# A second trunk that starts 16 steps earlier beside a stream of expert rows, its gated blocks first

## The chip, the cores and the metric

The kernel runs on one core of a Trainium2 chip. The metric is the device time of one execution in microseconds. All tensors are float32.

## What is computed

One inference step of a two-layer decoder for two groups of tokens (512 prompt rows, 64 sample rows). Each layer adds three things to the residual rows `x`: a mixer, a cross-attention, and PEER, a lookup of single-neuron experts:

```
q = t @ w_pq                                  # 8 heads, 2 halves of 128
s1, i1 = top_k(s[:, :, 0], 16); s2, i2 = top_k(s[:, :, 1], 16)     # s = q @ sub_keys
cand = s1[..., :, None] + s2[..., None, :]; top_s, pos = top_k(cand, 16)
idx = (i1 * 128 + i2)[pos]; g = softmax(top_s)                     # 128 experts per row
out = sum_e g[e] * gelu(t . peer_u[idx[e]]) * peer_v[idx[e]]
```

The mixer multiplies one normed input by `w_in` (seven parts of 1024 columns: b, c, h for a short convolution, u and v for the gated branch, and two gates), then by three more 1024x1024 matrices. `v` goes through gelu and a layernorm, `u` through gelu.

## The kernel before

**Trunks and the stream.** The work is cut into four passes `p`: for each of two layers, tiles 0 and 1 (256 rows), then tiles 2, 3 and 4 (320 rows). The dense part of a pass is its *trunk*; its PEER part is a stretch of one long *stream*. A *pick* `m` is one of the 128 experts of each of a tile's 128 rows: POOL (GpSimd) gathers the 128 rows of `peer_u` (one indirect DMA of 512 KB into one of eight `urow` slots) and of `peer_v` (another into one of eight `vrow` slots). Pass 0 has picks 0 to 255, pass 1 the next 320, 1152 in all. The trunk of pass 1 runs beside the stream of pass 0, and so on. Only trunk 0 has no stream beside it.

**A step of the stream.** At step `m` DVE (VectorE) computes `dot(m)`, a product and row sum of `urow` with the normed row, at line 1781. ACT makes weights (`w_done`) of four dots at a time. The weighted row of pick `m - LAG` (`LAG` = 8) is added either on DVE (`sum_up`, line 1797) or on PE (TensorE), as two matmuls with a diagonal matrix (line 1049). `plan_sums` gives picks 0 to 39 to PE, and 40 to 200 to DVE. POOL goes in order: before `urow` of pick `m` it waits for dot `m - 8`, before `vrow` of pick `v` for the sum of pick `v - 8`, which frees the slot.

**What sets the order.** Each engine's order is fixed when the program is written. `phase_jobs` lists the matmul jobs of a trunk, `places` gives each a step of the stream (`AHEAD`; `STARTS` is the place of the job ahead of it). An engine that comes to a job calls `peer_to(place)` first and so does the stream's work up to that step. PE does this at the end of each job with the `STARTS` of the next one, and only for its sums. DVE and ACT do it ahead of taking a job's result (line 1520 is ACT's copy out of a PSUM bank), so a result that is ready early stays in its bank until its step, and for one that is late the engine waits with the stream behind it. On DVE, `v` is taken `LATE_GELU` = 4 steps after its place.

**The start.** Trunk 0 ends with the scores (`sc`) of eight heads. In the second half of this tail, blocks of two queries (`pq`) and one score alternate, with scores of heads 2 to 7 at steps 5, 11, 15, 19, 24 and 29. The top-k of tile 0 (`top_group`) goes by head groups 0, 1, 2-3, 4-5 and 6-7, in nine parts each, within the windows between these steps. Trunk 1 begins at step `FIRST` = 40 with `par` (a transpose of parameter rows, whose DMAs SP issues once score 7 is done), norms (`n`), `v`, then blocks c, h, b, u twice, with `lg` and `lb` (layernorm rows spread over the partitions by PE, line 1112) behind the first c. DVE takes `lg` at step 61 and `lb` at step 63. The top-k of tile 1 (`top_k`, in 18 parts) is spread over steps 40 to 104.

**Weights.** SP (SyncE) loads them in units of 2 MB into two slots of `W`, in order; a unit is loaded when PE has finished the unit two before it.

Of the kernel before, what the change touches and what calls it, by code (L numbers as in the profile page):

```python
# [25 lines left out]
KC = DM // P  # L26
# [15 lines left out]
BLK = 4  # L42
# [9 lines left out]
FIRST = 40  # L52
HEAD = 40
# [51 lines left out]
def topk_window(p, i):  # L105
# [7 lines left out]
    return step_base(p) + FIRST, step_base(p) + FIRST + WIDE  # L113
# [27 lines left out]
def first_tail():  # L141

    jobs = [(at[:-1], "dve" if at[0] == "xo" else "act", 2 if at[0] in ("xo", "sk", "n") else 1, 1) for at in FIRST_TAIL]
    for h in range(2, PH):
        jobs += [(("pq", c), "act", 1, 1) for c in queries_before(h)] + [(("sc", h), "act", 2, 1)]
    return jobs


def phase_jobs(p):
# [23 lines left out]
    if not p:  # L173
        jobs += [(("sw",), "dve", 2, 1)]
    for a in range(2):
        jobs += block("c", a, "act")
        if a == 0 and p:
            jobs += [(("lg",), "dve", 2, 1), (("lb",), "dve", 2, 2 * nt)]
        jobs += block("h", a, "dve") + block("b", a, "dve") + block("u", a, "act")
# [69 lines left out]

def places(p):  # L250
# [4 lines left out]
    if p == 0:  # L255
        score = {("sc", h): (0, 0, 5, 11, 15, 19, 24, 29)[h] for h in range(PH)}
# [5 lines left out]
    begin, end = step_base(p - 1) + (FIRST if p == 1 else LAG + 2), step_base(p)  # L262
    if p % 2:
# [80 lines left out]
def plan_units(index):  # L344
# [10 lines left out]
    for p in range(2 * DEPTH):  # L355
        g = p % 2
        nt = len(GROUPS[g])
        for n in range(2):
            add(p, "v", n, "v", nt - 1)
        for a in range(2):  # L360
            for kind in "chbu":
# [74 lines left out]
def decoder_step(nc, A, O):  # L436
# [20 lines left out]
    with ExitStack() as ctx:  # L457
# [312 lines left out]
        def head_window(p, k):  # L770

            ends = [AHEAD[p, "sc", h + n - 1] for h, n in head_groups(p)] + [FIRST if p == 0 else step_base(p) + CARRY if carries(p) else step_base(p) - OVER]
# [186 lines left out]
        def _(pool):  # L959
# [31 lines left out]
            for m in range(STEPS_IN_ALL):  # L991
                if m == NU:
                    pool.wait_ge(job_done, JOB[0, "xo", 1] + 1)
                    for v in range(NV):
                        gather_values(v)
# [6 lines left out]
                if m >= LAG + NV:  # L1002
# [4 lines left out]
        def _(pe):  # L1007
# [186 lines left out]
            def trunk(p):  # L1194
# [33 lines left out]
                for a in range(2):  # L1228
                    for kind in "chbu":
                        for c in range(BLK * a, BLK * a + BLK):  # L1230
                            project((p, kind, c), c, hT)
                        if kind == "c" and a == 0 and p:
                            pe.wait_ge(ln_in, 32 * (p + 1))
                            spread((p, "lg"), LN_ROW, 2 * KC, 0)
                            spread((p, "lb"), LN_ROW, 2 * KC, KC)
# [147 lines left out]
                for h in range(0 if p else 2, PH):  # L1383
                    for c in queries_before(h):
# [18 lines left out]
        def _(act):  # L1403
# [52 lines left out]
            asides += [(step_base(1) - 8, copy_beside, ())]  # L1456
            asides.sort(key=lambda a: a[0])
# [64 lines left out]
            def trunk(p):  # L1522
# [55 lines left out]
                n = ncols(g)  # L1578
                if p:
                    act.wait_ge(idx_done, turns_to(p - 1, len(GROUPS[(p - 1) % 2]) - 1 if g == 0 else 0))  # L1580
                for a in range(2):
                    for c in range(BLK * a, BLK * a + BLK):
                        evac((p, "c", c), F1[:, c, 0:n], pf((p, "c", c)))
                    for c in range(BLK * a, BLK * a + BLK):
                        evac((p, "u", c), F2[:, c, 0:n], pf((p, "u", c)), ACT.Gelu_apprx_tanh)
# [123 lines left out]
                for h in range(0 if p else 2, PH):  # L1709
                    for c in queries_before(h):  # L1710
# [8 lines left out]
                    for k, (h0, some) in enumerate(head_groups(p)):  # L1719
                        if k and h == h0 + some - 1:  # L1720
                            group_exps(p, k - 1)
                k = len(head_groups(p)) - 1
                peer_to(head_window(p, k)[1] - 1)
                group_exps(p, k)
# [13 lines left out]
        def _(dve):  # L1738
# [91 lines left out]
            asides, going = [(p, i) for p in range(2 * DEPTH) for i in range(1, len(GROUPS[p % 2]))], []  # L1830

            def aside_to(n):

                while asides:
                    p, i = asides[0]
                    if not going:
                        going.append([0, top_k(p, i)])
                    k, work = going[0]
                    if topk_steps(p, i, k) > n:
# [143 lines left out]
            def top_group(p, k):  # L1983
# [3 lines left out]
                first, after = head_window(p, k)  # L1987
                at = [0]

                def breathe():  # L1990
                    at[0] += 1
                    peer_to(first + round((after - first) * at[0] / SEGS))

# [15 lines left out]
                breathe()  # L2009
# [4 lines left out]
                breathe()  # L2014
                each(lists, lambda a: dve.max_index(i16[:, a, 8:16], m16[:, a, 8:16], part[a]))
                candidates(all_cand, h, n)
                breathe()
                each(heads, lambda a: dve.max(tops[:, a, 0:8], cand[a]))
                each(heads, lambda a: dve.max_index(pos[:, a, 0:8], tops[:, a, 0:8], cand[a]))
                breathe()  # L2020
# [330 lines left out]
```

## Time and profile before

| | |
|---|---|
| median of 3 runs | 4121.95 us (4120.48 to 4128.55) |
| the profiled execution | 4122.23 us, span 4120.4 us |
| busy share of the span | PE 80%, DVE 71%, POOL 64%, ACT 25% |
| moved by DMA | 1522.37 MB, 369 GB/s over the span |
| gathers | 1152 of `peer_u`, 1152 of `peer_v`, 1208 MB |

The profile's span is the time from the first to the last instruction; the measured time is 1.8 us longer. The page cuts the span into 40 slices of 103 us. The first gather is issued at 434 us, the last dot of pass 0 comes at about 1370 us.

### The profile page before, as it was taken

How to read it: one execution, taken by the hardware profiler on the slowest of the kernel's cores; microseconds unless marked ns; L12 is line 12 of the kernel's file. 1: busy time of each engine (PE TensorE's matmuls, PEld its weight loads, DVE VectorE, ACT ScalarE, POOL GpSimd, SP SyncE). 2: the span in 40 equal slices, each digit the busy share in tenths (PEclk: the TensorE clock that was granted, in tenths of full speed). 3: DMA queues.
4: the chain of work that ended last, by engine and by line, in shares of the span. 5: the costliest groups of instructions: out<-in, count | busy, mean ns of one | idle time of the engine just before them, and what ended most of it. 6: DMA issues, size and time to landing. Idle time of an engine off the chain costs nothing. (4 is left out here: it accounts for less than half of the span.)

```text
span 4120.4 us, 37106 instructions
## 1 busy us (share of the span) xinstructions
PE 3280.7 (80%) x11224; PEld 1951.2 (47%) x11224; DVE 2929.9 (71%) x5930; ACT 1011.3 (25%) x2939; POOL 2642.7 (64%) x2318
## 2 busy tenths in 40 slices
PE   9999989899789798775858768897777866756666
PEld 6876646665545236664344426664544422222211
DVE  2110589987668878787776779997767777676654
ACT  1001331121323321122223421121313322221233
POOL 0000476676567677787677686777757777777775
PEclk9999999999899899887979879898889989988877
DMA  6445799999999999999999989999899999999998
GB/s 222 143 143 194 272 348 387 371 403 407 374 403 408 383 402 405 403 404 407 409 405 403 401 309 397 405 403 406 351 404 405 409 408 408 402 411 409 409 410 336
DMA packets 462382, 1522.37 MB, mean 369 GB/s; under 512 B 41220, under 2 KB 45604, under 8 KB 462184
## 3 DMA queue, kind: packets, MB, share of 16 engines
q0 software_dynamic: 331776, 1208.11, 74.6%
q1 hardware_dynamic: 130408, 311.90, 20.1%
q8 instruction: 91, 1.49, 0.1%
q14 instruction: 107, 0.88, 0.1%
HBM read 1512.62 MB, written 7.23 MB: 369 GB/s over the span
## 5 line engine op out<-in xcount | busy, mean ns | idle before, releaser
L981 POOL DMA_INDIRECT urow<-in_peer_u_dram,idx x1152 | 1341.3, 1164 | 1022.5 <-DVE idx L1913 438.0
L981 POOL DMA_INDIRECT vrow<-in_peer_v_dram,idx x1152 | 1299.2, 1128 | 438.4 <-issue 316.7
L1049 PE MATMUL ps<-vrow,diag 128*128 128x512 f32 (+1 forms) x2068 | 988.3, 692 | 398.0 <-DMA vrow<-in_peer_v_dram,idx 352.9
L1076 PE MATMUL ps<-RH,W 128*128 128x256 f32 (+1 forms) x4544 | 1179.5, 422 | 127.5 <-DMA W<-in_w_in_dram 45.4
L1076 PEld LDWEIGHTS ps<-RH,W 128*128 128x128 f32 x4544 | 894.8, 198 | 419.3 <-issue 99.7
L1781 DVE CUSTOM_DVE_ANT_0 urow<-urow,T 128x1024 f32<-128x1024 f32 x712 | 869.2, 1223 | 207.7 <-DMA urow<-in_peer_u_dram,idx 166.0
L1797 DVE SCALAR_TENSOR_TENSOR X<-vrow,wts,X 128x1024 f32<-128x1024 f32 x590 | 758.9, 1286 | 133.8 <-issue 119.2
L1049 PEld LDWEIGHTS ps<-vrow,diag 128*128 128x128 f32 (+1 forms) x2068 | 334.0, 196 | 1001.1 <-issue 796.0
L1781 DVE CUSTOM_DVE_ANT_0 urow<-urow,ps 128x1024 f32<-128x1024 f32 x376 | 456.2, 1218 | 282.6 <-DMA urow<-in_peer_u_dram,idx 278.2
L1480 ACT ACTIVATE gel<-dots 128x4 f32<-128x4 f32 x288 | 58.9, 205 | 1859.9 <-DVE dots L1781 1837.1
L1076 PE MATMUL ps<-RB,W 128*128 128x256 f32 (+1 forms) x1024 | 256.2, 411 | 11.1 <-DVE RV L2212 5.6
L1498 ACT ACTIVATE diag<-ident,wts 128x128 f32<-128x128 f32 (+1 forms) x645 | 224.5, 372 | 129.1 <-PE ps L1049 125.0
L1482 ACT ACTIVATE wts<-gel,gate 128x1 f32<-128x1 f32 x1152 | 245.1, 283 | 9.3
L1076 PEld LDWEIGHTS ps<-RB,W 128*128 128x128 f32 x1024 | 197.0, 193 | 68.2 <-DVE RV L2212 6.4
L1098 PE MATMUL ps<-W,RV 128*128 128x512 f32 (+1 forms) x320 | 132.5, 619 | 43.2 <-DVE RV L2218 43.2
L1098 PE MATMUL ps<-W,RB 128*128 128x512 f32 (+1 forms) x384 | 160.4, 614 | 5.1 <-DVE RB L2141 3.3
L1098 PE MATMUL ps<-W,RH 128*128 128x512 f32 (+1 forms) x320 | 129.1, 600 | 16.4 <-DVE RH L2070 15.5
L1098 PEld LDWEIGHTS ps<-W,RB 128*128 128x128 f32 (+1 forms) x384 | 67.0, 188 | 95.9 <-issue 90.8
L1480 ACT ACT_TABLE_LOAD x76 | 97.5, 1283 | 59.6 <-issue 31.8
L1098 PEld LDWEIGHTS ps<-W,RV 128*128 128x128 f32 (+1 forms) x320 | 55.1, 188 | 118.7 <-issue 74.1
L1520 ACT ACTIVATE RB<-ps 128x256 f32<-128x256 f32 (+2 forms) x130 | 50.9, 417 | 243.6 <-PE ps L1076 217.5
L1520 ACT ACTIVATE RV<-ps 128x320 f32<-128x320 f32 (+4 forms) x110 | 48.0, 447 | 251.4 <-PE ps L1076 199.0
(271 smaller groups left out, 2311.1 us busy)
## 6 DMA issues: line engine op xcount, KB each, us to landing
W<-in_w_in_dram SPq DMA_DIRECT2D x56, 2048.0 KB, 18.9
W<-in_w_pq_dram SPq DMA_DIRECT2D x16, 2048.0 KB, 19.0
urow<-in_peer_u_dram,idx POOLq DMA_INDIRECT x1152, 16.4
vrow<-in_peer_v_dram,idx POOLq DMA_INDIRECT x1152, 16.4
W<-in_w_a_out_dram SPq DMA_DIRECT2D x8, 2048.0 KB, 18.9
W<-in_w_b_out_dram SPq DMA_DIRECT2D x8, 2048.0 KB, 19.2
W<-in_w_mix_o_dram SPq DMA_DIRECT2D x8, 2048.0 KB, 14.1
W<-in_w_xq_dram SPq DMA_DIRECT2D x8, 2048.0 KB, 19.2
```

Of the source, the lines that this page charges most:

```text
L981: return pool.indirect_dma_start(ring[:, slot, :], None, table, bass.IndirectOffsetOnAxis(ap=idx[:, q % TSLOT, e:e + 1], axis=0))
L1049: o = pe.matmul(out, diag[:, pe_turn[m] % NDIAG, 0:rows], vrow[:, m % NV, b * 512:(b + 1) * 512], start=m in pe_first, stop=m in pe_last)
L1076: m = pe.matmul(pf(name), slot(u)[:, k, c % BLK * P:c % BLK * P + P], src[:, k, 0:ncols(name[0] % 2)], start=(k == 0), stop=(k == KC - 1))
L1098: m = pe.matmul(out, src[:, k, i * P:i * P + rows], row_slot((p, kind, n))[:, k % 4, a * 512:(a + 1) * 512], start=(k == 0), stop=(k == KC ...
L1480: ch.link(act.activation(gel[:, :], dots[:, at, :], ACT.Gelu_apprx_tanh))
L1482: w = act.activation(wts[:, at, j:j + 1], gel[:, j:j + 1], ACT.Copy, scale=gate[:, q % TSLOT, e + j:e + j + 1])
L1498: made = act.activation(diag[part, pe_turn[m] % NDIAG, 0:rows], ident[part, part], ACT.Copy, scale=wts[part, m // GRP % WRING, m % GRP:m % ...
L1520: act.activation(out, in_, func).then_inc(act_evac, 1)
L1781: dve.tensor_tensor_reduce(urow[:, m % NU, :], urow[:, m % NU, :], rows, 1.0, 0.0, ALU.mult, ALU.add, dots[:, n % WRING, m % GRP:m % GRP + ...
L1797: dve.scalar_tensor_tensor(out=out, in0=vrow[:, m % NV, :], scalar=wts[:, m // GRP % WRING, m % GRP:m % GRP + 1], in1=base, op0=ALU.mult, ...
```

## The change

Four things, all for pass 0 and trunk 1:

1. The queries and scores of heads 2 to 7 are issued in blocks (two queries and two scores, then twice four queries and two scores) at steps 0, 4 and 8.
2. Their top-k leaves the trunk's own order: groups 2-3, 4-5 and 6-7 become asides of the stream, spread over steps 8 to 20, 20 to 36 and 36 to 52. The top-k of tile 1 has steps 54 to 112.
3. Trunk 1 begins at step 24 (`SECOND`). Behind `v` come both u blocks, with `lg` and `lb` behind the first (DVE takes them at steps 53 and 56), and from step 62 (`GATED`) on c, h, b twice. Everything behind has its place 1 to 4 steps earlier than before, and the same place from step 197 on.
4. POOL gathers `vrow` of picks 0 to 7 one by one behind `urow` of picks 8 to 15, no longer all eight ahead of `urow` of pick 8.

Which picks PE sums (0 to 39) doesn't change, nor does any instruction's size or number.

```diff
+SECOND = 24
+GATED = 62
+FIRST_WINDOWS = ((0, 0), (0, 8), (8, 20), (20, 36), (36, 52))
+INLINE = 2
@@ topk_window
-    return step_base(p) + FIRST, step_base(p) + FIRST + WIDE
+    return step_base(p) + FIRST_WINDOWS[-1][1] + 2, step_base(p) + FIRST + 72
@@ phase_jobs
+    for a in range(2 if p == 1 else 0):
+        jobs += block("u", a, "act")
+        if a == 0:
+            jobs += [(("lg",), "dve", 2, 1), (("lb",), "dve", 2, 2 * nt)]
     for a in range(2):
         jobs += block("c", a, "act")
...
+def queries_of(p, h):
+
+    if p:
+        return queries_before(h)
+    return () if h % 2 else tuple(range(2 * h + (2 if h == 2 else 0), 2 * h + 4))
@@ places
-        score = {("sc", h): (0, 0, 5, 11, 15, 19, 24, 29)[h] for h in range(PH)}
+        score = {("sc", h): (0, 0, 0, 0, 4, 4, 8, 8)[h] for h in range(PH)}
...
-    begin, end = step_base(p - 1) + (FIRST if p == 1 else LAG + 2), step_base(p)
-    if p % 2:
+    begin, end = step_base(p - 1) + (SECOND if p == 1 else LAG + 2), step_base(p)
+    if p == 1:
+        stretches = [(0, early, begin, GATED), (early, late, GATED, end - CLOSE)]
+    elif p % 2:
@@ block.gpsimd
             for m in range(STEPS_IN_ALL):
-                if m == NU:
+                if m == LAG:
                     pool.wait_ge(job_done, JOB[0, "xo", 1] + 1)
-                    for v in range(NV):
-                        gather_values(v)
...
-                if m >= LAG + NV:
+                if m >= LAG:
                     gather_values(m - LAG)
@@ block.scalar
+            asides += [(first + (after - first) * 6 // SEGS + 1, group_exps, (0, k)) for k, (first, after) in enumerate(FIRST_WINDOWS) if k]
...
+                if p == 1:
+                    evac_gated(range(KC))
+                    peer_to(AHEAD[p, "c", 0])
@@ block.vector
+            asides[:0] = [(0, -k) for k in range(INLINE, len(FIRST_WINDOWS))]
...
+                if i > 0:
+                    return topk_steps(p, i, k)
+                first, after = FIRST_WINDOWS[-i]
+                return first + round((after - first) * k / SEGS)
...
-                breathe()
+                yield
...
-                for k in range(0 if p else 1, len(head_groups(p))):
-                    top_group(p, k)
-                weigh_group(p, len(head_groups(p)) - 1)
+                for k in range(0 if p else 1, len(head_groups(p)) if p else INLINE):
+                    heads_inline(p, k)
+                if p:
+                    weigh_group(p, len(head_groups(p)) - 1)
```

PE, from the query block of head 3 in trunk 0's tail on, before (L1076 is a block of queries, L1391 scores, L1049 sums of the stream, two matmuls for a pick, `ident,PAR` is `par`, the first job of trunk 1):

```order
L1076 MATMUL ps<-RH,W 128x256 x16
L1391 MATMUL ps<-KV,RV 128x128 x4
L1049 MATMUL ps<-vrow,diag 128x512 x6
L1076 MATMUL ps<-RH,W 128x256 x16
L1391 MATMUL ps<-KV,RV 128x128 x4
L1049 MATMUL ps<-vrow,diag 128x512 x8
...
L1049 MATMUL ps<-vrow,diag 128x512 x10
L1391 MATMUL ps<-KV,RV 128x128 x4
L1065 MATMUL ps<-ident,PAR 128x48
L1049 MATMUL ps<-vrow,diag 128x512 x32
```

The same place in the changed kernel, where the lines are L1097 (queries), L1411 (scores), L1086 (`par`) and L1070 (sums):

```order
L1097 MATMUL ps<-RH,W 128x256 x16
L1411 MATMUL ps<-KV,RV 128x128 x8
L1097 MATMUL ps<-RH,W 128x256 x32
L1411 MATMUL ps<-KV,RV 128x128 x8
L1097 MATMUL ps<-RH,W 128x256 x32
L1411 MATMUL ps<-KV,RV 128x128 x8
L1086 MATMUL ps<-ident,PAR 128x48
L1070 MATMUL ps<-vrow,diag 128x512 x32
```

Sixteen sums (picks 0 to 15) that stood between the score blocks stand behind `par` now. Before, sixteen others stood there (picks 16 to 31).

PE again, in the changed kernel, from the last rows of `v` (L1119) to `lg` and `lb` (L1133), with the first u block (L1097, four chunks of 8 matmuls):

```order
L1119 MATMUL ps<-W,RH 128x512 x10
L1119 MATMUL ps<-W,RH 64x512 x8
L1070 MATMUL ps<-vrow,diag 128x512 x14
L1097 MATMUL ps<-RH,W 128x320 x8
L1070 MATMUL ps<-vrow,diag 128x512 x2
L1097 MATMUL ps<-RH,W 128x320 x24
L1133 MATMUL ps<-GV,ident 128x128 x16
```

The last eight sums of picks 0 to 39 stand behind `v`, seven of them ahead of the first u chunk; before, all forty were done in the first third of `v`.

## Rows read from the trace of the kernel before

**Rows 1.** The page: DMA busy tenths and rate in 40 slices of 103 us

```profile
DMA  6445799999999999999999989999899999999998
GB/s 222 143 143 194 272 348 387 371 403 407 374 403 408 383 402 405 403 404 407 409 405 403 401 309 397 405 403 406 351 404 405 409 408 408 402 411 409 409 410 336
```

**Rows 2.** Windows: length, PE, PEld, DVE, ACT, POOL busy, clock, DMA share, GB/s

```profile
440.00:500.00 60.00, 54.89 (x255) 44.03 (x256) 36.34 (x129) 17.34 (x51) 34.05 (x31) 0.94 0.98 366
...
555.00:600.00 45.00, 36.23 (x116) 17.67 (x115) 39.30 (x116) 18.19 (x55) 36.94 (x27) 0.92 0.90 328
...
725.00:785.00 60.00, 56.11 (x221) 39.74 (x222) 58.97 (x163) 9.18 (x29) 37.63 (x32) 1.00 1.03 403
...
1016.00:1086.00 70.00, 57.60 (x314) 43.56 (x313) 48.11 (x65) 29.09 (x60) 36.54 (x30) 0.93 0.92 363
```

**Rows 3.** Windows again, cut at 647 and 848 us

```profile
647.00:848.00 201.00, 187.22 (x720) 132.96 (x719) 192.84 (x423) 29.52 (x92) 125.98 (x103) 0.97 1.00 379
848.00:1371.00 523.00, 451.83 (x1734) 280.03 (x1734) 398.96 (x754) 155.35 (x397) 345.84 (x287) 0.92 1.01 395
```

**Rows 4.** Windows of the dots' line alone (two records a dot): DVE busy, records

```profile
439.00:647.00 208.00, 74.51 (x122) 0.95 0.97 359
647.00:848.00 201.00, 63.00 (x103) 0.97 1.00 379
```

**Rows 5.** Waits of DVE and of POOL, 440 to 600 us

```profile
DVE m L2007 <- ACT KV L1717: 22.0, 3, 10.0
DVE urow L1781 <- DMA urow<-in_peer_u_dram,idx: 15.6, 2, 15.3
...
POOL vrow L981 <- PE ps L1049: 25.5, 12, 5.8
```

**Rows 6.** Waits of DVE, 600 to 800 us, and 1000 to 1160 us

```profile
DVE urow L1781 <- PE ps L1112: 5.0, 1, 5.0
...
DVE rmax L2243 <- PE ps L1292: 19.6, 1, 19.6
```

**Rows 7.** Timeline of PE, 440 to 655 us: start, duration, [idle before]

```profile
468.27 8.83 PE L1076 MATMUL ps<-RH,W 128*128 128x256 f32 x32 [2.79 <-DMA W<-in_w_pq_dram]
476.93 1.05 PE L1391 MATMUL ps<-KV,RV 128*128 128x128 f32 x8
...
492.49 7.03 PE L1049 MATMUL ps<-vrow,diag 128*128 128x512 f32 x16
...
537.60 0.34 PE L1065 MATMUL ps<-ident,PAR 48*128 48x48 f32 x1 [6.13 <-DMA PAR<-in_conv_w_dram]
...
594.91 5.39 PE L1098 MATMUL ps<-W,RH 128*128 128x512 f32 x12 [0.66 <-DVE RH L2070]
...
607.00 26.41 PE L1098 MATMUL ps<-W,RH 128*128 128x512 f32 x76
633.48 17.46 PE L1076 MATMUL ps<-RH,W 128*128 128x320 f32 x64
650.87 3.83 PE L1112 MATMUL ps<-GV,ident 16*128 16x128 f32 x32
```

**Rows 8.** Timelines of POOL and DVE around the first gathers

```profile
434.26 1.09 POOL L981 DMA_INDIRECT urow<-in_peer_u_dram,idx  x1 [431.13 <-DVE idx L1913]
481.70 0.94 POOL L981 DMA_INDIRECT vrow<-in_peer_v_dram,idx  x1 [5.80 <-PE ps L1049]
...
439.38 1.22 DVE L1781 CUSTOM_DVE_ANT_0 urow<-urow,T 128x1024 f32<-128x1024 f32 x1
```

**Rows 9.** Groups of DVE by line, 566 to 850 us: busy, mean ns

```profile
L1781 DVE CUSTOM_DVE_ANT_0 urow<-urow,T 128x1024 f32<-128x1024 f32 x76 | 92.5, 1220 | 7.5 <-PE ps L1112 5.0 <-DMA urow<-in_peer_u_dram,idx 1.6 <-DVE RV L2125 0.3
L1797 DVE SCALAR_TENSOR_TENSOR X<-vrow,wts,X 128x1024 f32<-128x1024 f32 x65 | 83.7, 1287 | 2.0 <-issue 2.0
...
L1941 DVE FIND_INDEX8 i<-m,KV 128x8 uint16<-128x128 f32 x16 | 4.2, 282 | 0.0
...
L1940 DVE MAX8 m<-KV 128x8 f32<-128x128 f32 x16 | 3.3, 272 | 0.0
```

More of the change, by code:

```diff
@@ L359, in plan_units @@
             add(p, "v", n, "v", nt - 1)
+        for a in range(2 if p == 1 else 0):
+            add_block(p, "u", a)
         for a in range(2):
-            for kind in "chbu":
+            for kind in "chb" if p == 1 else "chbu":
                 add_block(p, kind, a)
@@ L770, in head_window @@
         def head_window(p, k):
-            ends = [AHEAD[p, "sc", h + n - 1] for h, n in head_groups(p)] + [FIRST if p == 0 else step_base(p) + CARRY if carries(p) else step_base(p) - OVER]
+            if p == 0:
+                return FIRST_WINDOWS[k]
+            ends = [AHEAD[p, "sc", h + n - 1] for h, n in head_groups(p)] + [step_base(p) + CARRY if carries(p) else step_base(p) - OVER]
             return ends[k], ends[k + 1]
@@ L1227, in trunk @@
                     gating_transposes()
[L1228 to L1235, printed above, removed]
+                for kind, a in ([("u", 0), ("u", 1)] if p == 1 else []) + [(kind, a) for a in range(2) for kind in ("chb" if p == 1 else "chbu")]:
+                    for c in range(BLK * a, BLK * a + BLK):
+                        project((p, kind, c), c, hT)
+                    if p and (kind, a) == ("u" if p == 1 else "c", 0):
+                        pe.wait_ge(ln_in, 32 * (p + 1))
+                        spread((p, "lg"), LN_ROW, 2 * KC, 0)
+                        spread((p, "lb"), LN_ROW, 2 * KC, KC)
                 if g:
@@ L1383, in trunk @@
                 for h in range(0 if p else 2, PH):
-                    for c in queries_before(h):
+                    for c in queries_of(p, h):
                         project((p, "pq", c), c, hT)
@@ L1578, in trunk, with evac_gated @@
                 n = ncols(g)
+                def evac_gated(some):
+                    for c in some:
+                        evac((p, "u", c), F2[:, c, 0:n], pf((p, "u", c)), ACT.Gelu_apprx_tanh)
+                if p == 1:
+                    evac_gated(range(KC))
+                    peer_to(AHEAD[p, "c", 0])
                 if p:
@@ L1583, in trunk @@
                         evac((p, "c", c), F1[:, c, 0:n], pf((p, "c", c)))
-                    for c in range(BLK * a, BLK * a + BLK):
-                        evac((p, "u", c), F2[:, c, 0:n], pf((p, "u", c)), ACT.Gelu_apprx_tanh)
+                    if p != 1:
+                        evac_gated(range(BLK * a, BLK * a + BLK))
                 if g:
@@ L1719, in trunk @@
                     for k, (h0, some) in enumerate(head_groups(p)):
-                        if k and h == h0 + some - 1:
+                        if p and k and h == h0 + some - 1:
                             group_exps(p, k - 1)
-                k = len(head_groups(p)) - 1
-                peer_to(head_window(p, k)[1] - 1)
-                group_exps(p, k)
+                if p:
+                    k = len(head_groups(p)) - 1
+                    peer_to(head_window(p, k)[1] - 1)
+                    group_exps(p, k)
             for p in range(2 * DEPTH):
@@ L2035, in top_group, with heads_inline @@
                 expert_ids(marks, h, n, idx[:, kept, where], layer_of(p)).then_inc(idx_done, n)
-                breathe()
+                yield
                 if k and not carries(p):
                     weigh_group(p, k - 1)
+                if p == 0 and k == len(FIRST_WINDOWS) - 1:
+                    weigh_group(p, k)
+            def heads_inline(p, k):
+                first, after = head_window(p, k)
+                for at, part in enumerate(top_group(p, k)):
+                    peer_to(first + round((after - first) * (at + 1) / SEGS))
             def trunk(p):
```

39 lines of the change are left out of this document (20 added, 19 removed).

## The prediction

> **What bounds the kernel now.** The page first. From the sixth slice on, the DMA engines are busy nine tenths or more almost everywhere, at some 405 GB/s; the slices before the ninth move 194, 272, 348 and 387 [rows 1]. A gather pair is 1.05 MB, so 2.6 us a step at 405 GB/s, and a unit of weights (2.1 MB) is 5.2 us. Bytes are the same in both kernels, so a gain can only come from stretches in which DMA is not full. They are seen in the windows: 366 GB/s from 440 to 500 us, 328 from 555 to 600, 363 from 1016 to 1086, against 403 in between [rows 2].
>
> But DMA isn't alone. From 647 to 848 us DVE is busy 192.8 of 201 us, and 5.0 of the 8 idle ones are one wait at the start, for `lg` and `lb` from PE [rows 3, 6]. It makes steps 61 to 112 in that time: 122 records of dots before 647, 103 behind, two a dot [rows 4]. So up to step 112 a DVE that stands still is time lost, though the bytes would allow a catch-up; behind 848 us it idles 124 of 523 us and DMA sets the pace [rows 3]. PE is the third: 187.2 of 201 us.
>
> Then what DVE waits for at the start: 22.0 us for scores (the S copies in KV), 15.6 us for `urow`, of which 15.3 at once [rows 5]. POOL waits 25.5 us in 12 pieces for PE's sums, the longest 5.8 [rows 5]: short ones, since PE sums three to five picks between two score blocks.
>
> **The waits that the change removes.** With `urow` of pick 8 ahead of all `vrow`, the 15.3 us wait goes. The scores of head 3 come right behind its queries, at about 466 us in place of 478, since the block of two queries (7.1 us) that stood at 468 goes behind. DVE comes to them at 456, so it waits 10 us there. The later score waits, 22.0 us less what is left, go as well: scores 4 to 7 are ready long before steps 20 and 36. Removed: some 37 us of DVE idleness, 10 put back.
>
> **The wait that takes its place.** PE's order shows all 16 first sums behind `par`. From 468.3 us PE has four query blocks of two queries (8.8, then three of 7.1), and four scores in two pairs of 1.05 [rows 7]: 468.3 + 30.1 + 2.1 = 500.5 us. Only then does SP issue the parameter rows, for which PE waited 6.1 us before [rows 7]; so `par` is at 507 and the first sum ends at 509 (a sum is 7.03 / 4 = 1.76 us, [rows 7]). POOL's ninth `vrow` gather, at 481.7 us before [rows 8], is at about 510, and `urow` of pick 17 stands behind it in POOL's order. Behind it, a first dot comes 5.1 us after the issue (434.3 to 439.4, [rows 8]), so dot 17 is at 517. What DVE has until then: from 466 us, dots 8 to 16 (9 x 1.22 = 11 us, [rows 9]) and two thirds of the top-k of heads 2 and 3 (some 9 us), to 488. It then idles 29 us. So of the 37 us removed, 39 come back, and at 517 us DVE has made 17 steps.
>
> The Trainium skill (DMA: Bandwidth & Descriptors, Queues, rings and completion order) says that on each DMA engine descriptors are consumed in ring order. The second `v` unit, which SP issues a microsecond ahead of the parameter rows, would then stand in front of them with all its 2 MB. Before, that unit was issued 10 us ahead of them, so the 6.1 us don't show it; by the rule the wait for `par` would be 8 us and the sum below 2 us more.
>
> **The next bound: PE up to `lg` and `lb`.** From 507 us PE has: 40 sums, 70 us; norms and transposes, 7; `v`, 35 (six matmuls in 5.4 us and 38 in 26.4, the last four at 0.9, [rows 7]); the first u block, priced as the c block, 17.5; `lg` and `lb`, 3.8 [rows 7]. That is 133 us, with some 9 us of waits for norms and late `vrow`: 649 us, `lg` 2 us earlier. Before, `lb` ended at 654.7 [rows 7]. PE is thus 6 us ahead. But DVE takes `lg` at step 53, not 61, and stands there with the stream until 647. It comes there early: dots and the top-k groups bring it to step 45 at about 593; it waits 6 us for `v`; the 14 matmuls at the end of `v` hold no sum, so the ring of `vrow` stands, and the sum of pick 40, DVE's own, comes 6 us late; then step 53 at 631 and 15 us for `lg`. These new waits are 27 us, instead of the 8 that DVE idled from 647 to 848 [rows 3] and the little before.
>
> **The sum.** At 647 us DVE is at step 53 where it was at 61. Eight steps at 1.22 + 1.29 us [rows 9] are 20 us. The top-k of tile 1 begins at 54, not 40, so by then a third of its 18 parts is not done: 16 MAX8 at 3.3 us, 16 FIND_INDEX8 at 4.2, a third round as long, half of a fourth [rows 9], 13 us. The merge at step 60 is 1 us. Against this, it goes on 6 us earlier. Everything else up to step 112 is the same work, with DVE never idle in it: step 112 is 28 us later, at 876.
>
> Something comes back. PE isn't held by DVE until all eight PSUM banks wait, so it runs up to two blocks ahead of the places, and weights are loaded ahead with it. By its own work (eleven units of 17.5 us, the waits for each and `mx`) it is at 880 us 1.75 units further than before at 848: 9 us of DMA that step 112 to 256 no longer need. There DMA is the bound, and the 19 us that remain stay to the end: no later instruction of the stream moves. In numbers: 4122.2 + 28 - 9 = 4141 us. The profiled execution is within 0.3 us of the median, so that holds for the median too.
>
> Edits at no cost: blocks c, h, b behind u (PE's and ACT's work is the same, and ACT is busy 29.5 of 201 us [rows 3]); the top-k groups as asides (the same instructions, their identities ready at steps 19, 34 and 50, eight or more before POOL needs them at 24, 56 and 88, or nearly so for the first); the order of the first gathers, whose bytes are full pace either way.
>
> **Unknown costs.** The wait for `par`: from 2.8 us (PE's wait for weights, [rows 7]) to 15.3 (the longest wait for a DMA in these rows, [rows 5]), so -3 to +9. The 9 us of PE waits, none to twice that. The new waits before `lg` can't cost less than nothing. The credit for weights lies between 0 and two units, 10 us. Taken together, since not all ends fall on one side, -16 to +19 around 4141; I take the middle, since each piece comes from rows nearby.
>
> **The rivals.**
>
> *Bytes alone decide (no change), 18%.* The DMA engines lose time against 403 GB/s before 665 us in both, and what one kernel loses at 490 to 517 us the other lost at 470 to 520 and 575 to 600. If DVE is less bound than its busy time says (some of its waits hidden in long instructions), it catches up, as 403 GB/s are there in both. Then 4122 us, within 8. For it: DMA stands at 1.03 where DVE is full [rows 2]. Against it: 61 steps at 647 us become 53, and that is 8 MB that have to come later, of which the units ahead hold only half.
>
> *The gaps are filled (faster), 22%.* Trunk 1's start is moved to where DMA isn't full, and the waits of the start go. From 439 to 647 us the rate is 359 GB/s [rows 4], against 403 a loss of 208 x 44/403 = 23 us; at 1016 to 1086 another 7 [rows 2], where DVE waits 19.6 us for scores that PE brings late [rows 6], and a PE two blocks ahead might bring early. If half of these 30 us is gained, the time is 4107 us. It decides if PE's first sum ends before 490 us, or if DVE reaches step 53 with `lg` there. Against it: PE's order, and that the 19.6 us follow from the distance of `mo` to the scores, which keeps its 13 steps or so.
>
> The Trainium skill (Perfetto Trace Analysis, Optimization Strategy) speaks for this one: where the most contended engine changes over time, interleaving the regimes may improve performance. It would have the early trunk fill the early gaps, for the 4107 us just given; the order on PE speaks against it here.
>
> *Slower, by 8 to 38 us, 60%:* the forecast.
>
> **How the numbers follow.** A measurement of this kernel tells 0.2%, 8 us, from no change. Faster 22%, the same 18%, slower 60%. The likeliest case has its own range from 4130 (below it the time is the same) to 4160. The range over all reaches down into the faster case to leave a tenth out on either side: 4106 to 4160.
>
> **What the profile would show.** Right: `par` near 507 us, a train of 16 sums behind it, POOL idle some 25 us or more for PE at `vrow` and DVE idle about 29 us for `urow` near 490 to 517; DVE waiting over 8 us for `lg`; 53 dots at 647 us; no score wait above 12 us; step 112 near 876 us; the stretch from step 256 on as before, only later. Wrong: a first sum before 490 us, `lg` ahead of step 53, DVE idle by over 10 us between `lg` and step 112 (then DVE isn't the bound there), or a gap at the scores of trunk 1 that is gone.

## The result, and the profile after

| | before | after |
|---|---|---|
| median | 4121.47 us (4118.15 to 4128.55, 6 runs) | 4140.83 us (4139.06 to 4141.91, 6 runs) |
| ratio | | 1.0043, 95% interval 1.0033 to 1.0054 |
| span of the profiled execution | 4120.4 us | 4138.5 us |

The change costs 19 us. The ratio, here and below, is estimated from all executions, with its interval; the quotient of the two medians is 1.0047. The page of the kernel after has the same bytes, and the rate is lower in the fifth slice (225 GB/s) than in [rows 1] (272):

```profile
DMA  5445699999999999999999989999999999999998
GB/s 215 149 143 193 225 340 377 370 387 406 369 407 407 395 406 406 402 404 407 409 404 393 408 304 395 404 404 407 364 405 405 409 409 409 406 411 409 409 410 335
```

The windows of after, with the columns and the edges of [rows 2]:

```profile
440.00:500.00 60.00, 55.37 (x303) 49.60 (x302) 38.65 (x135) 13.82 (x36) 26.89 (x23) 0.97 0.85 318
555.00:600.00 45.00, 42.26 (x113) 17.65 (x112) 35.05 (x105) 11.83 (x39) 36.16 (x30) 0.96 0.91 321
725.00:785.00 60.00, 57.37 (x214) 40.27 (x213) 59.02 (x159) 5.63 (x24) 37.95 (x31) 1.00 1.01 389
1016.00:1086.00 70.00, 58.57 (x241) 43.89 (x242) 48.87 (x65) 25.33 (x59) 33.65 (x28) 0.85 0.92 357
```

No gap is filled: 366 GB/s at 440 us has become 318, and the gap at 1016 us is there as before (357). The waits of DVE and POOL from 440 to 600 us, to be read beside [rows 5]:

```profile
DVE urow L1811 <- DMA urow<-in_peer_u_dram,idx: 43.4, 12, 30.3
DVE m L2038 <- ACT KV L1746: 9.6, 1, 9.6
...
POOL vrow L1004 <- PE ps L1070: 41.1, 4, 40.2
```

The score waits have shrunk from 22.0 to 9.6 us, and one wait of 30.3 us has taken the place of the 15.3. The timeline of POOL tells what is behind it:

```profile
472.66 0.94 POOL L1004 DMA_INDIRECT urow<-in_peer_u_dram,idx  x1 [0.30 <-issue]
513.75 0.94 POOL L1004 DMA_INDIRECT vrow<-in_peer_v_dram,idx  x1 [40.16 <-PE ps L1070]
514.99 0.94 POOL L1004 DMA_INDIRECT urow<-in_peer_u_dram,idx  x1 [0.30 <-issue]
```

POOL stands for 40 us with the ninth `vrow` gather, for PE's first sum, and the next `urow` gather stands behind it. PE's timeline, as in [rows 7]:

```profile
485.18 1.95 PE L1411 MATMUL ps<-KV,RV 128*128 128x128 f32 x16
486.96 13.98 PE L1097 MATMUL ps<-RH,W 128*128 128x256 f32 x64
500.78 1.95 PE L1411 MATMUL ps<-KV,RV 128*128 128x128 f32 x16
509.43 0.34 PE L1086 MATMUL ps<-ident,PAR 48*128 48x48 f32 x1 [6.71 <-DMA PAR<-in_conv_w_dram]
509.70 28.45 PE L1070 MATMUL ps<-vrow,diag 128*128 128x512 f32 x60
...
607.12 12.33 PE L1119 MATMUL ps<-W,RH 128*128 128x512 f32 x36
619.38 12.28 PE L1070 MATMUL ps<-vrow,diag 128*128 128x512 f32 x28
...
637.52 13.08 PE L1097 MATMUL ps<-RH,W 128*128 128x320 f32 x48
650.54 3.83 PE L1133 MATMUL ps<-GV,ident 16*128 16x128 f32 x32
```

`par` comes at 509.4 us and a row of sums (PE adding weighted rows of picks) right behind it. And `lb` ends at 650.54 + 3.83 = 654.4 us, where it ended at 654.7 before. DVE, from 600 to 800 us, is to be read beside [rows 6]:

```profile
DVE urow L1811 <- PE ps L1133: 8.6, 1, 8.6
DVE bns L2152 <- ACT RV L1580: 7.3, 2, 4.0
DVE urow L1811 <- DMA urow<-in_peer_u_dram,idx: 7.2, 4, 3.1
```

Last, the dots' line in windows, as in [rows 4] (two records a dot), first of after, then of before with its edge at the same point of the trunk:

```profile
439.00:647.00 208.00, 64.86 (x106) 0.96 0.90 329
```

```profile
439.00:653.00 214.00, 74.56 (x123) 0.95 0.97 360
```

The dot of step 53 starts at 652.6 us in after, right behind `lg`; in before that of step 61 starts at 653.0. From there 229 us to step 112 (881.4 us; 847.7 before, so 33.7 later). At step 256 after is 20.5 us behind (1392.1 against 1371.6), at the end 18.

### The profile page after: what moved, and what is told of

It reads as the page before. It is cut to its first block and busy times, and to the rows that moved or that the text cites. A ratio compares the mean times of both kernels' runs of the same rounds, so it can differ in the third digit from the quotient of the medians.

```text
span 4138.5 us, 37105 instructions
## 1 busy us (share of the span) xinstructions
PE 3275.3 (79%) x11224; PEld 1939.8 (47%) x11224; DVE 2930.4 (71%) x5930; ACT 1013.1 (24%) x2939; POOL 2640.4 (64%) x2318
## 5 line engine op out<-in xcount | busy, mean ns | idle before, releaser
L1070 PE MATMUL ps<-vrow,diag 128*128 128x512 f32 (+1 forms) x2068 | 988.6, 694 | 397.0 <-DMA vrow<-in_peer_v_dram,idx 347.8
L1097 PE MATMUL ps<-RH,W 128*128 128x256 f32 (+1 forms) x4544 | 1173.6, 420 | 127.6 <-DMA W<-in_w_in_dram 43.5
L1097 PEld LDWEIGHTS ps<-RH,W 128*128 128x128 f32 x4544 | 890.8, 197 | 416.2 <-issue 87.6
L1070 PEld LDWEIGHTS ps<-vrow,diag 128*128 128x128 f32 (+1 forms) x2068 | 331.2, 195 | 1005.1 <-issue 789.7
L1097 PE MATMUL ps<-RB,W 128*128 128x256 f32 (+1 forms) x1024 | 257.7, 413 | 11.9 <-DVE RV L2253 5.6
L1097 PEld LDWEIGHTS ps<-RB,W 128*128 128x128 f32 x1024 | 198.1, 194 | 69.4 <-DVE RV L2253 6.5
L1119 PE MATMUL ps<-W,RV 128*128 128x512 f32 (+1 forms) x320 | 132.8, 620 | 64.0 <-DVE RV L2259 64.0
L1119 PE MATMUL ps<-W,RB 128*128 128x512 f32 (+1 forms) x384 | 160.4, 614 | 6.3 <-DVE RB L2182 3.4
L1119 PE MATMUL ps<-W,RH 128*128 128x512 f32 (+1 forms) x320 | 134.1, 614 | 19.7 <-DVE RH L2109 18.5
L1119 PEld LDWEIGHTS ps<-W,RV 128*128 128x128 f32 (+1 forms) x320 | 55.1, 188 | 139.8 <-issue 74.4
L1119 PEld LDWEIGHTS ps<-W,RB 128*128 128x128 f32 (+1 forms) x384 | 67.0, 188 | 97.0 <-issue 91.5
L1811 DVE CUSTOM_DVE_ANT_0 urow<-urow,RV 128x1024 f32<-128x1024 f32 x64 | 78.1, 1225 | 43.7 <-DMA urow<-in_peer_u_dram,idx 42.0
## 6 DMA issues: line engine op xcount, KB each, us to landing
W<-in_w_mix_o_dram SPq DMA_DIRECT2D x8, 2048.0 KB, 14.6
```

The costliest lines, as they stand in the source:

```text
L1070: o = pe.matmul(out, diag[:, pe_turn[m] % NDIAG, 0:rows], vrow[:, m % NV, b * 512:(b + 1) * 512], start=m in pe_first, stop=m in pe_last)
L1097: m = pe.matmul(pf(name), slot(u)[:, k, c % BLK * P:c % BLK * P + P], src[:, k, 0:ncols(name[0] % 2)], start=(k == 0), stop=(k == KC - 1))
L1119: m = pe.matmul(out, src[:, k, i * P:i * P + rows], row_slot((p, kind, n))[:, k % 4, a * 512:(a + 1) * 512], start=(k == 0), stop=(k == KC ...
L1811: dve.tensor_tensor_reduce(urow[:, m % NU, :], urow[:, m % NU, :], rows, 1.0, 0.0, ALU.mult, ALU.add, dots[:, n % WRING, m % GRP:m % GRP + ...
```

## What each stretch of DVE says

The reading that all the experiments were compared by: DVE's busy time between its first dot and step 112. Windows of DVE alone (length, busy, records), first before, then after:

```profile
439.40:847.70 408.30, 349.97 (x903) 0.96 0.98 369
```

```profile
441.80:881.40 439.60, 350.52 (x905) 0.95 0.94 352
```

The work is the same 350 us. The stretch is 31.3 us longer, and all of that is idle time: 58.3 us before, 89.1 after. It is worked out as length less busy time, here and for every run below. The other 2.4 us of the 33.7 lie ahead of the first dot (441.8 against 439.4 us). They are no part of the change: the runs e1 to e4 below, which are the same up to there, have their first dots at 438.9 to 439.8.

One profiled execution is one sample, and two of the runs below show how far samples differ. e3 is the same program as the change up to step 63, e4 up to step 119. Their `lb` ends at 648.0 and 649.9 us (654.4 in after), and from the first dot to step 64 DVE idles 82.6 and 84.7 us (86.4 in after). In e4 step 112 comes at 876.9 us with 87.4 us idle (881.4 and 89.1 in after). So a difference of 4 us or less between two profiles says little by itself.

The theory in three parts. (1) PE sets when `lb` is there, 648 to 655 us in the profiles of both kernels and of e3 and e4. (2) Up to then DVE makes no more than the steps placed ahead of `lg`: 53, not 61. (3) Behind it DVE is full up to step 112, so that what is missing at `lg` is missing there; from there DMA sets the pace. Rival A: the 30 us stall at the start is the cause by itself. Rival B: only what DMA carries counts.

## The experiments

The runs were measured in four batches, and each is compared with the kernel before in the same batch. In two of them it took 4120.9 us (e1 to e4, chip number 6 in the record) and 4121.1 us (e9 and e10, number 5); in the other two 4238.5 us (e5 to e8, number 7) and 4240.5 us (e11 and e12, number 5 once more). The last two are called the slower batches here; there ratios are compared, and only among themselves. The expectations were written for 4121 us. Some of them speak of a chip that is unlike the others; what the record has on that is in the last section.

**e1: sums between the score blocks.**

```diff
-        score = {("sc", h): (0, 0, 0, 0, 4, 4, 8, 8)[h] for h in range(PH)}
+        score = {("sc", h): (0, 0, 0, 0, 12, 12, 20, 20)[h] for h in range(PH)}
```

> The changed kernel, but the second query/score block stands at step 12 and the third at step 20 (4 and 8 in the change), so that PE makes sums between the score blocks and not sixteen in a row behind `par`. Theory (PE sets the time up to `lg` and `lb`, the stall at the start only moves the idle time): DVE's 30.3 us wait for urow is under 8 us and POOL's 40.2 us wait for PE's sums under 12 us, but `lb` on PE ends at 654 us as before (650 to 657), since PE has the same work ahead of it; DVE stands longer at `lg` (over 20 us in place of 8.6) and step 64 and step 112 are where they were (881 us, within 4). Time 4141 less 0 to 5 us. Rival A (the stall at the start is the cause by itself): all of the 30 us that DVE idles are worth time; step 112 comes 20 to 30 us earlier, the time is 4111 to 4121. Rival B (bytes alone): the gathers get going 30 us earlier and carry 8 to 10 MB more by 555 us, which DMA needs no more later: 4120 to 4130.

4142.78 us, ratio 1.0054 (1.0040 to 1.0067): nothing gained, and 2 us above the expected range. DVE's waits from 440 to 700 us:

```profile
DVE urow L1811 <- DMA urow<-in_peer_u_dram,idx: 29.8, 7, 13.0
DVE bns L2152 <- ACT RV L1580: 16.7, 2, 9.8
DVE rstd L2093 <- ACT PARC L1541: 12.7, 1, 12.7
DVE m L2038 <- ACT KV L1746: 9.6, 1, 9.6
DVE urow L1811 <- PE ps L1133: 8.7, 1, 8.7
```

The single wait of 30 us is gone, though not as far as expected: the longest wait for urow is 13.0 us (under 8 said), POOL's longest for PE's sums 17.8 (under 12 said). And the idle time up to step 112 is 88.8 us where it was 89.1 in after. It went to `par`, which comes 21 us later on PE (530.6 us), and to the rows of `v`, not to `lg`, where over 20 us were expected. `lb` ends at 651.6 us. Rival A falls for the kernel with `lg` at 53.

**e2: the parameter rows early.** They are loaded behind the third query unit, not behind the second `v` unit.

```diff
             def load_vectors(p):
-                load_early(p)
+                if p > 1:
+                    load_early(p)
@@ SP, behind a unit
+                if u == (0, "pq", 2):
+                    load_early(1)
```

> The changed kernel, but the parameter rows of trunk 1 (`par`) are loaded right behind the third query unit of trunk 0 and not behind the second `v` unit. PE's 6.7 us wait for `par` must go. Theory (PE bound up to `lg`): everything of PE up to `lb` is 6 to 7 us earlier (648 us in place of 654), step 112 5 to 7 us earlier, the time 4134 to 4137. Rival A (stall alone): DVE's wait of 30.3 us is 7 us shorter, the same time as the theory; the two differ in the first experiment. Rival B (bytes): a few kilobytes sooner change nothing in what DMA must carry, 4140, within 2.

4133.57 us, 1.0031 (1.0019 to 1.0043): 12.7 us above the kernel before in place of 19.4, so 7 us are back. (The two intervals overlap, but the slowest of its six executions took 4136.3 us and the fastest of the change's 4139.1.) The timeline of PE:

```profile
500.95 0.26 PE L1089 MATMUL ps<-ident,PAR 48*128 48x48 f32 x1
501.14 19.15 PE L1073 MATMUL ps<-vrow,diag 128*128 128x512 f32 x44
...
640.86 3.83 PE L1136 MATMUL ps<-GV,ident 16*128 16x128 f32 x32
```

PE has no wait for `par`. `lb` ends at 644.7 us, step 64 is at 687.6 and step 112 at 871.7: each 9.7 or 9.8 us earlier than in the profile of after, of which 2.8 are its first dot. Counted from the first dot, `lb` is 5.3 us earlier than in e4 and 3.4 earlier than in e3, so by the profiles alone the gain is 3 to 7 us. The parameter rows are 24 KB, and bytes moved a little earlier can't be worth that: rival B falls here.

**e3 and e4: a load on DVE at two places.** Behind each of 40 dots DVE fills the spent slot with zeros. The edit is that of e3; e4 has `120 <= m < 160` in its place.

```diff
-                dve.tensor_tensor_reduce(urow[:, m % NU, :], urow[:, m % NU, :], rows, 1.0, 0.0,
-                                         ALU.mult, ALU.add, dots[:, n % WRING, m % GRP:m % GRP + 1]).then_inc(u_read, 1)
+                product = dve.tensor_tensor_reduce(urow[:, m % NU, :], urow[:, m % NU, :], rows, 1.0, 0.0,
+                                                   ALU.mult, ALU.add, dots[:, n % WRING, m % GRP:m % GRP + 1])
+                if 64 <= m < 104:
+                    ch.link(product)
+                    product = dve.memset(urow[:, m % NU, :], 0.0)
+                product.then_inc(u_read, 1)
```

> The changed kernel with extra work on DVE that nothing needs: behind the dot of each of steps 64 to 103 the spent urow slot is filled with zeros (40 instructions over 128x1024). It measures the disputed point whether DVE sets the pace from `lg` to step 112. Their duration d isn't in any trace yet (between the 0.5 and the 1.3 us of the copies and products of that size). Theory (DVE is the bound there, as it was busy 193 of 201 us before and idles near 0 from 700 to 880 us now): step 112 comes later by all of 40 d (20 to 50 us), and nearly all of it stays to the end: 4141 + 0.7 to 1.0 x 40 d. Rival B (DMA sets the pace, DVE's waits hide in its instructions): under a third of 40 d is lost at the end.

> The same 40 instructions on DVE, but at steps 120 to 159, where DVE idled 124 of 523 us and DMA moves 400 GB/s. Theory: DMA is the bound there, so the load vanishes in DVE's idle time: 4141 to 4146 us, step 256 within 4 us of 1392. Beside the run with the load at steps 64 to 103 this gives what the same DVE time is worth in either stretch. Rival (DVE is bound everywhere): 4141 + 0.5 or more of 40 d, as in the other run.

The group of the added instructions is the same in both profiles:

```profile
L1815 DVE MEMSET urow<- 128x1024 f32 x40 | 36.5, 912 | 11.2 <-DVE dots L1811 11.2
```

So 36.5 us busy and 11.2 us in which DVE waits for its own dot: at most 47.7. DVE from step 64 to 112, in e4 (without a load there) and in e3 (with it):

```profile
692.90:876.90 184.00, 181.30 (x441) 0.96 0.99 377
```

```profile
691.00:917.50 226.50, 212.35 (x482) 0.86 0.88 313
```

This is 42.5 us longer. The times are 4178.17 us (1.0143) and 4150.50 us (1.0073): against their own runs of before +57.3 and +29.6, against the change's +19.4 that is 38 and 10 us. Of the 42.5 us, the load at steps 64 to 103 costs nine tenths to the end, though DMA was not full there (313 GB/s, where e4 has 377) and moved 393 GB/s from step 112 to 256; at steps 120 to 159 three quarters vanish. Part 3 of the theory holds, and rival B falls again. That 10 us stay in e4, and not 0 to 5, and that step 256 comes at 1401.9 us, 9.8 later and not within 4, is a miss: DVE's idle time there is not all where the load was put (steps 112 to 160 take 179.7 us, in the change 159.0).

**e5 and e9: `lg` seven steps later.**

```diff
-GATED = 62
+GATED = 70
```

> The changed kernel with GATED = 70 in place of 62: trunk 1 still begins with `par` at step 24, the sixteen sums still stand in a row behind it, and the u blocks still come first, but `lg` and `lb` are taken at steps 60 and 62 (53 and 56 in the change, 61 and 63 before) and c, h, b begin at 71. Theory (PE ends `lb` at 651 to 655 us whatever the steps are, and DVE makes only the steps placed ahead of it): DVE fills its idle time up to then with 7 more steps, so that step 64 comes about 14 to 17 us earlier than in the change (680 to 684 us), step 112 at 860 to 868, the time is 4124 to 4130. Rival A (the stall at the start is the cause): it is there unchanged, so 4138 to 4142. Rival B (bytes): 4138 to 4142 too, as nothing at the start moves.

> GATED = 70 once more, because the chip of the first attempt gave PE 144 us of idle time that waits for nothing the profile shows (none in the kernel before or after on its own chip), 15 us of it in `lg` and `lb`. On a chip without that idle time the theory expects `lb` on PE at 651 to 657 us, DVE there at step 60 with a wait under 8 us, step 64 at 678 to 686, step 112 at 860 to 870, and 4124 to 4131 us where the kernel before takes 4121. Rivals A and B (the stall at the start, or bytes, are the cause): 4138 to 4142.

In the slower batch (e5) 1.0036 (1.0020 to 1.0052). Its profile has PE at a stand for 15 us amid `lg` and `lb`, so it can't be judged by its steps (last section). In the later batch (e9) 4132.92 us, 1.0031 (1.0021 to 1.0042): 11.8 us above its own runs of before in place of 19.4, so 7.6 us better than the change; 2 above what was expected, and 5 below the 4138 to 4142 of the rivals, though one of its eight executions took 4141.0. `lb` ends at 652.2 us; the waits of DVE from 600 to 880 us:

```profile
DVE urow L1811 <- DMA urow<-in_peer_u_dram,idx: 10.0, 4, 3.5
DVE X L1827 <- DMA vrow<-in_peer_v_dram,idx: 0.9, 1, 0.9
```

There is no wait for `lg` any more. DVE comes to step 60 at 660.7 us, 8 us behind `lb`; step 61 is at 663.0 (688.2 in the change, 653.0 before), and the idle time up to step 112 is 76.5 us. It is 12.6 us less than in after, and 10.9 less than in e4: this is what it costs to have `lg` at step 53. The wait at `lg` itself was 8.6 us; the rest had lain at `v` and at urow.

**e8 and e10: both edits.** GATED = 70 and the diff of e2.

> The changed kernel with GATED = 70 and the early load of the parameter rows together. Theory: both act on the same bound (when PE has `lb`, and at which step DVE stands then), so their gains add up or nearly: the run with GATED = 70 less 4 to 7 us, 4118 to 4125, and the first candidate for beating the kernel before. Rival A: the early load is worth 7 us and the step of `lg` nothing: 4133.

> GATED = 70 with the early parameter rows once more, for the same reason. Theory: `lb` at 644 to 650 us, DVE hardly ahead of it, step 112 at 855 to 865, time 4117 to 4125. If the gains of both don't add up (4125 to 4131), DVE is late at step 60 itself and PE is no longer what it waits for.

In the slower batch (e8) 1.0014 (1.0000 to 1.0027), in the later one (e10) 4125.93 us, 1.0011 (1.0002 to 1.0020): one us above the expected range. `lb` ends at 645.1 us, step 64 is at 674.5 (673.0 before), step 112 at 857.3 (847.7). The idle time is 69.1 us. Three quarters of the loss (14.6 of 19.4 us) are back by two edits that leave the row of sums behind `par` as it is.

**e6: the trunk as it was.** Blocks c, h, b, u, `par` at step 40, `lg` at 61; all else as in the change.

```diff
-SECOND = 24
+SECOND = 40
+AHEAD_PASS = -1
@@ phase_jobs (and the same condition in places, add_block, and the orders of PE and ACT)
-    for a in range(2 if p == 1 else 0):
+    for a in range(2 if p == AHEAD_PASS else 0):
...
```

> The changed kernel with the trunk as it was: blocks in the order c, h, b, u, `par` at step 40, `lg` at 61. The score blocks at steps 0, 4 and 8, the top-k of heads 2 to 7 as asides, the windows of tile 1 and the order of the gathers stay as in the change. PE's sixteen sums still stand behind `par`. Theory: the stall at the start (DVE idle 29 us at 490 to 520) is there in full, but `lg` isn't early, so most of it is made up by 654 us, where DVE idled 5 to 13 us before: step 112 at 850 to 860, time 4122 to 4132. Rival A (the stall alone is the cause): 4136 to 4142. Rival B (bytes): 4120 to 4124.

The ratio is 1.0053 (1.0034 to 1.0073), which would be 4143 us where the kernel before takes 4121. The theory's 4122 to 4132 is missed, and it is rival A's time that came. PE, around the norms and `lb`:

```profile
509.54 0.34 PE L1087 MATMUL ps<-ident,PAR 48*128 48x48 f32 x1 [6.86 <-DMA PAR<-in_conv_w_dram]
...
604.02 1.06 PE L1087 MATMUL ps<-ident,RH 64*64 64x64 f32 x8 [13.61 <-DVE RH L2131]
...
679.15 3.83 PE L1134 MATMUL ps<-GV,ident 16*128 16x128 f32 x32
```

With the trunk at step 40 the stall doesn't stay on DVE. DVE comes to step 40 at 603.2 us (580.3 before), where it makes the normed rows, PE waits 13.6 us for them, and `lb` ends at 683.0, 28 us later than in either kernel. Part of that belongs to the slower batch: the nearest run there with this trunk, e7 below, ends `lb` at 660.4, and e6 is 23 us behind it. So part 1 of the theory holds only while the norms are placed early enough. It looks as if the early start keeps `lb` at 654 us under the stall, which the rest of the change (scores, asides, windows, gathers) brings.

**e7 and e12: edits to the kernel before.** e7 has the diff of e2 alone, e12 also the order of the first gathers:

```diff
-                if m == NU:
+                if m == LAG:
                     pool.wait_ge(job_done, JOB[0, "xo", 1] + 1)
-                    for v in range(NV):
-                        gather_values(v)
...
-                if m >= LAG + NV:
+                if m >= LAG:
                     gather_values(m - LAG)
```

> The kernel before with the parameter rows of trunk 1 loaded behind the third query unit of trunk 0 and nothing else changed. PE's wait for `par` (6.1 us) goes. Theory: `lb` ends at 648 to 650 us in place of 654.7, DVE's 5.0 us wait for `lg` goes, and little more can be had, because DVE then is late itself: 4115 to 4121. Rival B (bytes): 4121, within 2.

> The kernel before with two edits: the early parameter rows, and the change's order of the first gathers (urow of picks 8 to 15 ahead of the eight vrow). The trunk, the scores and the top-k stay as before, `lg` at step 61. DVE's 15.3 us wait for urow of pick 8 and PE's 6.1 us wait for `par` go. Theory: `lb` ends at 646 to 650 us (654.7 before), DVE is there at step 61, step 112 at 841 to 845 (847.7 before), and the time is 4114 to 4119, under the kernel before. If only one of the two, PE or DVE, is freed and the other still sets the time, 4119 to 4122. Rival B (bytes alone): 4121, within 2.

The ratios are 1.0009 (0.9994 to 1.0024) and 0.9992 (0.9975 to 1.0008), both in slower batches: no change that the measurement can tell. The gains that were expected, 0 to 6 us for e7 and 2 to 7 for e12, are too small for it. In e12 DVE's long wait for urow is gone as it should be, yet PE ends `lb` at 659.0 us, having waited 6.0 us for rows from DVE ahead of `v`; in e7 at 660.4. There is no run of these two in the other batches, and no profile of the kernel before in a slower one, so whether they would gain there stays open. No version was shown to beat the kernel before.

**e11: all three edits.** GATED = 70, the diff of e2 and the diff of e1.

> GATED = 70, the early parameter rows, and the second and third score blocks at steps 12 and 20, so all three edits at once. In the run with the first two DVE came to step 60 later than PE ended `lb` (no wait for `lg`, where the change has 8.6 us), so DVE's idle time at the start (23 us in one wait for urow) should now cost time, as it didn't when `lg` was at 53. Theory: the idle time in front of step 32 shrinks, step 64 comes at 664 to 672 us (674.5 without the third edit), the time is 4116 to 4123. If DVE only waits elsewhere for the same PE (for `par`, which comes later now, or for the rows of `v`), step 64 stays at 673 to 677 and the time at 4124 to 4128. Rival A (the stall at the start is worth its 20 to 30 us): 4100 to 4106.

The ratio is 1.0033 (1.0017 to 1.0049) against the 1.0014 of e8 in the other slower batch: no gain, if anything a loss. Idle time up to step 112 is 79.5 us, in e8 77.7. Step 64 comes at 684.9 us, in e8 at 685.5, so with `lg` at 60, too, sums between the scores only move the waits.

The runs side by side. Idle is DVE's idle time from the first dot to step 112, times in us:

| kernel | ratio | `lb` ends | step 64 | step 112 | idle |
|---|---|---|---|---|---|
| before | 1 | 654.7 | 673.0 | 847.7 | 58.3 |
| after | 1.0043 | 654.4 | 697.4 | 881.4 | 89.1 |
| e1 sums between | 1.0054 | 651.6 | 694.6 | 878.6 | 88.8 |
| e2 `par` early | 1.0031 | 644.7 | 687.6 | 871.7 | 82.3 |
| e9 GATED = 70 | 1.0031 | 652.2 | 682.2 | 865.0 | 76.5 |
| e10 both | 1.0011 | 645.1 | 674.5 | 857.3 | 69.1 |

## Why the prediction came out right, point by point

**The waits removed** held: score waits of 9.6 us (10 said), no 15.3 us wait.

**The wait in their place** held nearly to the number: `par` at 509.4 us (507), the first sum at once behind it, POOL's gather at 513.8 (510), DVE idle 30.3 us (29), POOL 40 us (over 25). The 2.4 us at `par` are the profiled execution's own: in e3 and e4, the same up to there, `par` comes at 506.0 and 507.1. By the ring order of the Trainium skill (DMA: Bandwidth & Descriptors, Queues, rings and completion order) the wait for `par` would have been 8 us. It was 6.7, with the second `v` unit issued at 501.0 us and the parameter rows from 502.8 on; from the last of these to the matmul it is 5.7 us (6.1 in e3), where it was 5.1 before with `v` 10 us ahead. So 0.6 to 1.0 us of the 2 were seen. In after the unit has landed at 508.7 us, ahead of the matmul, but in e4 and e9 the matmul comes 0.7 us ahead of the landing (507.1 against 507.8, 507.7 against 508.3): the parameter rows don't wait for the whole of the 2 MB.

**PE up to `lg` and `lb`** held, and is the centre of it: 649 us said for the end of `lb`, 654.4 measured in after, 648.0 and 649.9 in e3 and e4. e2 shows that PE sets this time. What the prediction had too simple was DVE's part: it counted 15 us at `lg`, 6 at `v` and 6 for late sums, and the profile shows 8.6 at `lg`, 7.3 at `v`, and 7.2 for urow: 23 us for 27. DVE came there later than thought, at step 45 at 611.6 us and not at 593. One reason is in the wait rows: beside the 30.3 us, DVE waits another 13.1 us in eleven pieces for urow up to 600 us (0.3 before), which the prediction put at nothing. Its own count of waits (39 for 37 removed, then 27 for some 8) makes 21 us and not the 28 of its sum; it is the sum, which goes by PE's time, that came out. And 18 matmuls (12.3 us) at the end of `v` hold no sum, not 14.

**The sum.** Eight steps, 53 for 61, is exact, and from DVE's release at `lg` to step 112 it took 229 us, as said (647 to 876). Step 112 itself came at 881.4 us, not 876, since `lg` was later; in e4, the same program up to there, it came at 876.9. That the missing work lies behind step 64 shows in the lengths from 64 to 112: 174.7 us before, 184.0 after, at the same idle time of 2.5 and 2.7 us. That is the 13 us term of the top-k of tile 1, as far as it isn't made up by step 64.

**What comes back** was 9 us by the prediction and 13.2 in the profile of after (33.7 at step 112, 20.5 at 256). By that profile two terms were too small and their misses nearly cancel, which is luck: +28 - 9 = +19 was said; +33.7 - 13.2 = +20.5 came at step 256, +18.1 at the end of the profiled execution and +19.4 in the medians. By e4's step 112, 29.2 us behind before, 10 us would come back to the medians' 19.4, and both terms were right. With one profile of the change, how much of it was luck stays open. The lengths from step 112 to 256 show that the credit is bounded, as the prediction's argument of units ahead has it: 523.9 us in before, 521.6 in e10, 518.6 in e9, 514.3 in e2, 510.6 in after, and no shorter, 511.3, in e3, where step 112 is another 36 us later. So at most 13 us came back in these profiles, where two units (10 us) were allowed for.

**The rivals.** That bytes alone decide falls with e2, where 24 KB loaded earlier are worth 7 us, and with e3. That the gaps are filled falls with the windows: from 439 to 647 us the rate is 329 GB/s, not 359. The interleaving of regimes that the Trainium skill advises (Perfetto Trace Analysis, Optimization Strategy) did not come about here, because the new work waited on PE, which was the busy one in that stretch (55.4 of 60 us and 42.3 of 45 in the windows of after).

**What the runs correct.** The prediction put the loss down to `lg` at step 53 and the delayed top-k together. By the runs, of 31 us of new idle time the place of `lg` is 12.6 (e9), the wait for `par`, which was there before as well, another 7.4 (e10); 10.8 are left. Each of these stands on one profile, with the scatter of some 4 us shown above; the medians, where 19.4 us of loss become 11.8 and 4.8, bear out the first two. Since DVE's work is the same and 8 us more of it lie behind step 64 in e9 and e10 too, the later windows of tile 1's top-k (54 to 112 for 40 to 104) are the likeliest source, DVE having had nothing else to do in its waits. No run had the old windows in the changed kernel, so this is argued and not shown. And by e6 the early start can't be all of the cause: without it the rest of the change costs as much (1.0053 in its batch, 1.0043 for the whole change in another, with intervals that overlap; the change itself was not run in a slower batch).

## What to carry to other kernels

Ask which engine sets the time at which a dependent job is there, and count how many steps of the other stream are placed ahead of that job: moving the job to an earlier step doesn't make it earlier, it only has the stream wait there with less done. A long wait in the table isn't a price: breaking up one of 30 us gained nothing, because the engine behind it was as busy as before. Where an engine does the same work in two kernels, compare its busy and idle time between two fixed steps; here that one pair of rows held the whole result.

## What the hardware showed unexpectedly

In two of the batches the kernel before took 4238.5 and 4240.5 us, 2.8 and 2.9% longer than in the others. This can't be put down to one bad chip: the record has number 7 for the first and number 5 for the second, and number 5 also for the batch 21 minutes earlier, where the same kernel took 4121.1 us. Either the numbers don't name the same chip each time, or the condition comes and goes; the record doesn't tell which. The mean granted clock of the executions was 0.88 to 0.89 there, and 0.89 to 0.91 elsewhere. The profiles of these batches show PE waiting for nothing that the profile names, here the waits of PE in e5 (a kind of row that no profile of the other batches has for PE):

```profile
PE ps L1070 <- DMA vrow<-in_peer_v_dram,idx: 226.4, 142, 7.2
PE ps L1070 <- issue: 144.4, 88, 10.7
```

At the sums of e6, e7, e8, e11 and e12 it is 159 to 193 us. In e5, e8 and e11 the small matmuls of `lg` and `lb` (32 records), 3.8 to 5.0 us in all other runs, took 23 to 24 us, many of them one at a time:

```profile
663.81 0.36 PE L1133 MATMUL ps<-GV,ident 16*128 16x128 f32 x1 [1.83 <-issue]
665.20 0.37 PE L1133 MATMUL ps<-GV,ident 16*128 16x128 f32 x1 [1.02 <-issue]
```

The page of e5 also has 366 to 376 GB/s in the 32nd to the 38th slice, where the kernel before had 402 to 411 in its own batch [rows 1]. What holds PE there was not tried. Filling 128x1024 floats with zeros took DVE 912 ns, three quarters of the 1220 ns of a product and sum over the same size.
